# Banded attention of a two-block network: VectorE scales one token block's weights after the sums and one after the next scores, GpSimd scales the other two; the output projection begins in bank 0

## What is computed

```
def band_rel_bias(table_h, block, dilation): ...      # a bias by distance, per head
s = einsum('bhgnqd,bhgnkd->bhgnqk', qb, kb) * (hd ** -0.5) + bias
s = where(mask, s, NEG_INF_2)
m = max(s, axis=-1)                  # with a sink for the last 8 heads
p = exp(s - m[..., None])
denom = sum(p, axis=-1)              # + exp(sink - m) for the last 8 heads
o = einsum('bhgnqk,bhgnkd->bhgnqd', p, vb) / denom[..., None]
...
return o @ w_out                     # the output projection, 1024 x 1024
```

## Time and profile before

| | |
|---|---|
| median of 3 runs | 2865.86 us (2861.12 to 2866.35) |
| the profiled execution, own time | 2864.47 us |
| its span | 2862.7 us |
| PE busy | 2719.8 us, 95% |
| DVE, ACT, POOL busy | 1463.3, 1213.8, 399.3 us |
| attention stage, first transpose to first matmul of the projection | 1341.90 to 1435.49 us |

### The profile page before, as it was taken

The page is one execution under the profiler, slowest core; times in us unless marked ns, Lnnn a source line. Parts: engine busy times, 40 slices in busy tenths (PEclk is TensorE's granted clock), DMA queues, the critical chain, the costliest instruction groups (busy, mean ns, idle before and its releaser), DMA issues. The chain is left out here.

```text
span 2862.7 us, 52104 instructions
## 1 busy us (share of the span) xinstructions
PE 2719.8 (95%) x22488; PEld 2157.3 (75%) x22488; DVE 1463.3 (51%) x2345; ACT 1213.8 (42%) x2071; POOL 399.3 (14%) x322
## 2 busy tenths in 40 slices
PE   8999999999999999999899999799898988899999
PEld 6877557688888888876478888677677776688887
DVE  3533774653443333345745243596678785453343
ACT  4322663632233222234634233375566755442232
POOL 0001551000000000021210000000354543100000
PEclk9998999999999999999999999899999998899999
DMA  4222002232323232232122322222000001332221
GB/s 181 94 74 89 1 1 96 70 132 93 118 75 117 96 103 89 96 131 71 41 102 103 103 90 102 103 74 90 10 10 8 8 8 34 118 111 91 101 100 62
DMA packets 38802, 228.53 MB, mean 80 GB/s; under 512 B 4352, under 2 KB 8448, under 8 KB 15024
## 3 DMA queue, kind: packets, MB, share of 16 engines
q1 hardware_dynamic: 32576, 201.34, 20.3%
q0 software_dynamic: 6000, 23.87, 2.4%
HBM read 220.93 MB, written 4.26 MB: 79 GB/s over the span
## 5 line engine op out<-in xcount | busy, mean ns | idle before, releaser
L446 DVE TENSOR_TENSOR weights_lo<-ring,weights_hi 128x1024 fp32r<-128x1024 f32 x347 | 427.2, 1233 | 692.6 <-ACT weights_hi L439 692.5
L439 ACT ACTIVATE weights_hi<-ring 128x1024 fp32r<-128x1024 f32 x364 | 382.5, 1053 | 569.7 <-PE bank L603 335.3
L495 PE MATMUL bank<-h_hi,weights_hi 128*128 128x512 f32 x384 | 150.1, 391 | 0.0
L601 PE MATMUL bank<-weights_hi,mlp_p_hi 128*128 128x512 f32 x384 | 149.6, 390 | 0.0
L496 PE MATMUL bank<-h_lo,weights_hi 128*128 128x512 f32 x384 | 149.5, 389 | 0.0
L602 PE MATMUL bank<-weights_lo,mlp_p_hi 128*128 128x512 f32 x384 | 149.4, 389 | 0.0
L603 PE MATMUL bank<-weights_hi,mlp_p_lo 128*128 128x512 f32 x384 | 149.4, 389 | 0.0
L497 PE MATMUL bank<-h_hi,weights_lo 128*128 128x512 f32 x384 | 149.4, 389 | 0.0
L2995 POOL TENSOR_TENSOR scan_b<-scan_a,scan_c 128x512 f32<-128x512 f32 x96 | 124.7, 1314 | 131.2 <-DVE scan_a L2969 109.4
L495 PE MATMUL bank<-mlp_h_hi,weights_hi 128*128 128x512 f32 x336 | 130.7, 389 | 0.0
L496 PE MATMUL bank<-mlp_h_lo,weights_hi 128*128 128x512 f32 x336 | 130.7, 389 | 0.0
(11 more groups left out here) (712 smaller groups left out, 6985.4 us busy)
## 6 DMA issues: line engine op xcount, KB each, us to landing
ring<-in_w_m SPq DMA_DIRECT2D x64, 1024.0 KB, 4.7
ring<-in_w_mb SPq DMA_DIRECT2D x24, 1024.0 KB, 4.7
ring<-in_w_fi SPq DMA_DIRECT2D x22, 1024.0 KB, 4.8
ring<-in_w_fo SPq DMA_DIRECT2D x10, 1024.0 KB, 4.9
ring<-in_w_a SPq DMA_DIRECT2D x7, 1024.0 KB, 5.0
attn_bias<-scratch POOLq DMA_DIRECT2D x16, 448.0 KB, 4.5
ring<-in_w_rg SPq DMA_DIRECT2D x5, 1024.0 KB, 4.9
ring<-in_w_v SPq DMA_DIRECT2D x4, 1024.0 KB, 11.2
```

What stands on the lines that cost most here:

```text
L439: act.e.activation(halves(g, s)[0], raw, ACT.Copy).then_inc(*act.up("act_unit_high", ("high", s)))
L446: lane.e.tensor_tensor(lo, raw, hi.bitcast(F32), ALU.subtract).then_inc(*lane.up(f"{lane.name}_unit_low", ("low", s)))
L495: pe.e.matmul(ps[:, :], hi, xh, start=k == 0, stop=False, skip_group_check=True)
L601: pe.e.matmul(ps[:, :], xh, hi, start=k == 0, stop=False, skip_group_check=True)
```

## The change

Three edits. POOL scales token blocks 2 and 3 of each pair in place of block 3 alone. DVE scales block 0 right after the reciprocals and block 1 only after the next scores (`dve_attn_scaled`); for pair 0, in the stage before, the two stand together. And PE sets the turn of the banks to 0 at the start of the output projection.

```
@@ dve_attn_in
     dve_attn_weights(g, dve, 0)
+    dve_attn_scaled(g, dve, 0, 1)
@@ dve_attn_weights
     dve.e.reciprocal(m[:, :, 4, :], m[:, :, 2, :]).then_inc(*dve.up("dve_weights", ("afactors", n)))
-    dve.wait_ge(dve.newest)
-    for qt in range(QT - 1):
-        for par in range(2):
-            pb = A.Pb[2 * (n % 3) + par][:, qt, slice(*keys(n, qt))]
-            dve.e.tensor_scalar(pb, pb, m[:, par, 4, qt:qt + 1], None, ALU.mult).then_inc(*dve.up("dve_weights", ("aweights_low", n)))
+    dve_attn_scaled(g, dve, n, 0)
+
+
+def dve_attn_scaled(g, dve, n, qt):
+    dve.wait_ge(g.at("afactors", n))
+    for par in range(2):
+        pb = g.A.Pb[2 * (n % 3) + par][:, qt, slice(*keys(n, qt))]
+        dve.e.tensor_scalar(pb, pb, g.A.nm[:, n % 3, par, 4, qt:qt + 1], None, ALU.mult).then_inc(
+            *dve.up("dve_weights", ("aweights_low", n)))
@@ dve_attn
             if i == 0 and n + 1 < NB:
                 dve_attn_weights(g, dve, n + 1)
+            if i == 1 and n + 1 < NB:
+                dve_attn_scaled(g, dve, n + 1, 1)
             if i == 1 and n:
                 dve_attn_low(g, dve, n - 1)
@@ pool_attn
-        for par in range(2):
-            pb = A.Pb[2 * (n % 3) + par][:, QT - 1, slice(*keys(n, QT - 1))]
-            pool.e.tensor_scalar(pb, pb, A.nm[:, n % 3, par, 4, QT - 1:QT], None, ALU.mult).then_inc(
-                *pool.up("pool_weights", ("aweights_high", n)))
+        for qt in (2, 3):
+            for par in range(2):
+                pb = A.Pb[2 * (n % 3) + par][:, qt, slice(*keys(n, qt))]
+                pool.e.tensor_scalar(pb, pb, A.nm[:, n % 3, par, 4, qt:qt + 1], None, ALU.mult).then_inc(
+                    *pool.up("pool_weights", ("aweights_high", n)))
@@ pe_attn_out
-    g.rotating = ROT
+    g.rotating, g.turn = ROT, 0
     pe_projected(g, pe, g.A.t, g.A.os)
```

## The result

The changed kernel takes 2857.09 us (median of 9 runs, 2853.05 to 2862.45), the kernel before on the same chip 2864.51 us (9 runs, 2861.02 to 2867.44). The ratio is 0.9977, with a 95% interval of 0.9967 to 0.9988, so 3.4 to 9.5 us are won, 7.4 by the medians. The profiled executions' spans differ by 8.1 us. Of the runs further down, one of e7 (3422 us) and one of the kernel before beside e5 to e8 (6847 us) lie far off and are left out of the intervals.

The account below looks back on a forecast made before the run. PE was taken as the bound, busy 95% of the span, idling in attention on late copies. Terms 2.47 + 0.2 + 0.91 + 0.65 + 1.48 = 5.7 us plus 1.2 for the clock gave 6.9, forecast 2858.5 us, range 2854.5 to 2862.5.

Parts of the forecast that it names:

- Term 1, pairs 1 and 2: Attention pairs 1 and 2: DVE reaches second scores sooner, so PE's waits of 1.69 and 0.78 us go; 2.47 us won.
- Pair 3's 0.2 us: Attention pair 3: a values piece 0.19 us longer than its twin was counted as 0.2 us won.
- Term 2, pairs 4 and 5: Attention pairs 4 and 5: DVE's shorter list removes PE's waits of 0.25 and 0.66 us for DVE's copies; 0.91 us won.
- Term 3, pairs 6 and 7: Pair 7 begins sooner, limited by POOL's four scalings; 0.65 us won, or 0.1 with POOL at its slow rate.
- Term 4, the bank: Start of output projection: with the turn at 0, PE's wait for pair 7's low part goes whole; 1.48 us won.
- The clock (+1.2): Half-clock stretch at pairs 4 and 5 may stay away; +1.2 us taken as likeliest, between -0.9 and +3.
- the second scores came within 1.5 us: Sign of being right at pair 1: DVE's second scores within 1.5 us of the reciprocals.
- pairs 1 and 2 lasted 12.88 and 12.55: Sign of being right: pair 1 lasts about 13.0 us and pair 2 about 12.4.
- POOL's fours of 128x512: Sign of being right: POOL's pieces of four scalings take 6.5 to 8.2 us.
- L601 follows without a gap: Sign of being right at the projection's start: L601 follows the last L2051 without a gap.
- PE waits for POOL at pair 7 alone, by under 1 us: Sign of being right: of all pairs, only pair 7 has PE waiting for POOL, under 1 us.
- strict turns on the shared port: Rival: DVE's first scalings wait for two of POOL's, 3.9 us in all; 2864.0 us; chance 0.10 shared with no action.

Follow-up runs that it names:

- e7: Changed kernel, but for pair 7 alone DVE also scales block 2 and POOL only block 3; median 2856.1 us, ratio 0.9964 to 0.9983 to the kernel before.
- e5: Changed kernel, but DVE scales blocks 0 and 1 together before the next scores; median 2859.3 us, ratio 0.9977 to 0.9995 to the kernel before.
- e8: Changed kernel with the new scalings for pairs 0 to 3 only, pairs 4 to 7 scaled as before; median 2857.2 us, ratio 0.9972 to 0.9990.
- e4: Changed kernel, but DVE keeps block 2, scaling blocks 1 and 2 after the next scores; POOL scales block 3 alone; median 2857.8 us, ratio 0.9975 to 0.9993.
- e1: Kernel before with only the bank turn set to 0 at the output projection; median 2861.9 us, ratio 0.9994 to 1.0011.
- e3: Changed kernel, but DVE waits for POOL's pair 7 scalings before the projection weights' low halves; median 2856.6 us, ratio 0.9972 to 0.9992 to the kernel before.
- e2: Changed kernel without the bank turn edit, so the scalings alone; median 2861.7 us, ratio 0.9987 to 1.0005 to the kernel before.
- e11: Changed kernel run once more, unchanged; median 2855.9 us, ratio 0.9966 to 0.9986 to the kernel before.
- e6: e3 plus ACT copying the second transposed set before the exponentials of pair n + 2's first scores; median 2852.8 us, ratio 0.9952 to 0.9976.
- e9: e6 without e3's wait, with e7's pair 7 and DVE copying the last transposed set earlier at pairs 4 to 6; median 2854.3 us, ratio 0.9959 to 0.9983.
- e10: Changed kernel with three low-half subtractions replaced by one-input instructions of the same size, low part left out; one run, stage 87.97 us against 86.63.
- e12: e9 run once more, on the same chip as e11; median 2852.7 us, ratio 0.9960 to 0.9984 to the kernel before.

## Why the prediction was right, and where it was not

The time came 1.4 us from the forecast. The mechanism of the two main terms, the second scores on DVE and the bank, is shown. That the sum came so near is luck in part: the change by itself is worth 4.4 us in the stage and not 5.7, one term has the wrong sign, and what fills the gap to the medians is not explained.

- **Term 1, pairs 1 and 2 (2.47 us)**: 1.76 + 0.61 = 2.37. The mechanism is shown by the rows of DVE and ACT above, and by e4 and e5, in which either way of reaching the second scores sooner removes most of it. Pair 3's 0.2 us did not come (12.56 both times).
- **Term 2, pairs 4 and 5 (0.91)**: too small. At the full clock the old scalings cost 2 x 0.86 = 1.72 us (e8). I took the waits that stood in the profile, 0.25 and 0.66 us. Without the slow stretch the first is 0.67 as well, and each costs 0.19 us more than its row shows, as said at e8. So the clock's part of the two pairs is 0.99 us, and the waits' is the larger one. I had put the clock at 1.4, and that was not even what my figures gave: 11.20 + 10.85 - 2 x 9.7 - 0.91 is 1.7.
- **Term 3, pairs 6 and 7 (0.65 won)**: wrong in sign. The step that failed is "For pairs 4 to 7 it is 2 x 1.24 + 2 x 1.05 = 4.6 us". That is what POOL takes for the pieces of pairs 4 to 6, but for pair 7's it is 6.28. I had counted what lies beside POOL in the other pairs, scalings, copies and bias-and-maximum, and overlooked that in pair 6 DVE goes on with the projection's low halves. PE waits 2.06 us, and pairs 6 and 7 together last 14.29 us in place of the 13.04 of e1 and e8, which begin the projection in bank 0 too: 1.25 us lost. e3 and e7 show the cause from two sides. A second, smaller step failed too. I let POOL start pair 7's piece 0.9 us sooner while pair 6 itself began 0.66 sooner; it started 2.45 us behind pair 6's first transpose, as before (2.46). So even with POOL undisturbed (e3) pair 6 is 0.31 us shorter than before and not 0.65.
- **Term 4, the bank (1.48)**: 1.54 us, by e1 and, the other way round, 1.58 by e2. The wait did not move elsewhere: none stands in e1's next 44 us, and behind the stage the same matmuls, taken in pieces of fifty where the clock was full, take by my estimate 0.6 us less in the twelve profiles with the turn at 0 than in the two without, with no place that stands out.
- **The clock (+1.2)**: in these two executions 2.57 us, which are 1.58 at pair 0, chance by e11, and 0.99 at pairs 4 and 5.

The sum of what the change does by itself in the stage is 1.76 + 0.61 + 1.72 - 1.25 + 1.54 = 4.4 us, where the prediction had 5.7. The medians say 7.4 and 6.9, with intervals that both hold 4.4. What the other 2 to 3 us are stays open. The slow stretch at pair 4, which two of three profiles with the old scalings there have and none of the eleven others, can be 0.99 us of them at most. The rest may be chance: when each kernel's stage is compared at the full clock, its median differs from what the stage gives by 1.8 us less (e2) to 3.0 us more (the changed kernel), by 1 us more on average over twelve measurements.

Of the signs named: the second scores came within 1.5 us, pairs 1 and 2 lasted 12.88 and 12.55 (13.0 and 12.4 said), POOL's fours of 128x512 took 6.6 to 6.8 us (6.5 to 8.2 said), L601 follows without a gap. "PE waits for POOL at pair 7 alone, by under 1 us" was wrong in its size. Of the rivals, strict turns on the shared port is refuted: DVE's first two scalings took 1.32 us beside POOL's, not 3.9.

## What to carry to other kernels

An in-order engine that empties banks for the critical one should touch what is waited for first, and do what is merely due for the next round behind it; that order alone was worth nearly as much as handing work to a third engine (3.2 against 3.6 us, e4 and e5) and had no price at pair 7, and it can be had again wherever a copy stands behind a chain (e6, e9). When work is handed to an engine, look at every round of the loop for what runs beside it and not at the typical one: the last round, where the next stage's preparation begins, turned 0.65 us forecast as won into 1.25 lost. Where a measurement can't tell 3 us from nothing, cut the trace at the program's own marks: the pairs repeat within 0.02 us, and what differs there is either the change or the clock.

## What the runs showed of the hardware

**POOL beside DVE.** A 128x256 scaling takes POOL 916 to 917 ns with nothing or DVE's copies out of banks beside it (e3), but 2515 ns beside DVE's 128x1024 subtractions of two SBUF tiles. Beside the form with one SBUF input the last two scalings take 3.1 us in place of 1.8 (e10). DVE hardly pays: the subtractions in the changed kernel, beside POOL, and then in e3, with POOL idle (least, median, most, in ns):

```profile
L446 DVE TENSOR_TENSOR weights_lo<-ring,weights_hi x3: 1207/1208/1410, 1421.3 to 1423.5; 128x1024 fp32r<-128x1024 f32 x3
```

```profile
L446 DVE TENSOR_TENSOR weights_lo<-ring,weights_hi x3: 1218/1220/1226, 1419.9 to 1422.2; 128x1024 fp32r<-128x1024 f32 x3
```

For the scalings of both engines: beside six of DVE's of 128x512 POOL takes 2.04 us for each of its own, beside four of DVE's 1.66 to 1.69 where they stand two and two, and 1.72 where they stand together (e5).

The Trainium skill ("SBUF — State Buffer", section "Who interferes with whom") says that a VectorE instruction with two SBUF inputs contends with a GpSimd one that reads SBUF, and that a scaling in the two-port mode does so too; this is the rule I did not apply to the low halves, and the trace agrees with its first part and e10 with the second, as far as e10's instruction ran in that mode, which no view shows. It also calls the shared pair an exclusive lock, and says of the two-port mode that whoever issues first holds the pair for the whole instruction while the other engine is blocked. The trace differs: POOL's last scaling ended within 2.5 us during which DVE's subtractions ran without a pause, so it lost 1.6 us and not all of it; the first subtraction began while a scaling of POOL's was still running and took 1207 ns, no more than with POOL idle; and DVE's two scalings at pair 1 were over after 1.32 us, before POOL's first, which began 0.07 us behind the first of them and took 1.84 us.

**The clock.** Pair 0, the same work of PE in all kernels, took 16.6 us with a granted clock of 0.90 in seven of fourteen profiles and 15.0 with 1.00 in the other seven, the changed kernel once each way. PE waits 1.98 or 1.99 us for a bank in that pair every time, also in the profiles that keep the full clock, so the wait alone does not decide. A slow stretch at pair 6 cost 0.93 us (8.54 against 7.61, e12 and e9). In the two profiles compared above such stretches are 2.57 of the 6.96 us by which the stages differ.
